# The rotary part of attention scores: two full passes become one full pass and a pair of 64-row passes

## The reference

```
q = concatenate([q_nope (128), rope(q_rope) (64)]);  k = concatenate([k_nope (128), rope(k_rope) (64, shared by the heads)])
s = einsum('bqhd,bkhd->bhqk', q, k) * scale
p = softmax(s);  out = einsum('bhqk,bkhd->bqhd', p, v)
```

## Time and profile before

| | us |
|---|---|
| runs of the kernel | 2785.1, 2790.86, 2793.07; median 2790.86 |
| span of the profiled execution | 2784.8 |
| median of the runs less that span | 6.1 |
| attention, from its first score matmul to its end | 829 to 1460 of the span |
| PE busy in the whole span | 2312.8 (83%) |
| PE, DVE, ACT, POOL busy in those 631 us | 606.0, 456.5, 355.7, 190.6 |

### The profile page before, as it was taken

One profiled execution on the slowest core, in us unless ns is written; L12 is line 12 of the kernel. 1 busy time (PEld: TensorE's weight loads), 2 busy tenths in 40 slices (PEclk: granted clock), 3 DMA queues, 4 the chain that ended last, 5 costly groups with the idle time before them and its releaser, 6 DMA issues. The chain is left out here.

```text
span 2784.8 us, 35274 instructions
## 1 busy us (share of the span) xinstructions
PE 2312.8 (83%) x11378; PEld 1915.8 (69%) x11378; DVE 1741.2 (63%) x2128; ACT 1102.2 (40%) x2062; POOL 1070.8 (38%) x711
## 2 busy tenths in 40 slices
PE   0899989999968999999988997949657765942998
PEld 0788868888856877787776885737546654732886
DVE  7233344444436777777762123799999999997432
ACT  2444433222225555555544555322332432341332
POOL 5222211222233333323311232747745855771444
PEclk9999989999989999999998998969878888975999
DMA  6333434434434333334214331010111011022553
GB/s 233 131 132 132 145 145 166 142 135 141 143 106 132 103 105 96 104 103 108 85 35 162 126 113 53 16 48 21 38 53 38 23 46 38 23 106 83 148 154 113
DMA packets 194607, 279.91 MB, mean 101 GB/s; under 512 B 10836, under 2 KB 139220, under 8 KB 189270
## 3 DMA queue, kind: packets, MB, share of 16 engines
q1 hardware_dynamic: 189910, 270.41, 30.2%
q10 hardware_dynamic: 4608, 8.39, 0.8%
HBM read 188.05 MB, written 90.70 MB: 100 GB/s over the span
## 5 line engine op out<-in xcount | busy, mean ns | idle before, releaser
L2062 DVE SCALAR_TENSOR_TENSOR conv_v<-u,par,conv_v 128x1024 f32<-128x1024 f32 x334 | 716.8, 2219 | 0.0
L2093 PE MATMUL ps<-ho_hi,wp_lo 128*128 128x512 f32 x768 | 314.3, 409 | 227.7 <-ACT gate L1985 164.8
L1950 POOL TENSOR_TENSOR conv_g<-conv_g,product 128x1024 f32<-128x1024 f32 x130 | 428.8, 3334 | 184.8 <-ACT product L1979 184.8
L2093 PEld LDWEIGHTS ps<-ho_hi,wp_lo 128*128 128x128 f32 x768 | 152.3, 198 | 266.0 <-issue 152.4
L2094 PE MATMUL ps<-h_left,wp_hi 128*128 128x512 f32 x768 | 310.8, 405 | 0.0
L2095 PE MATMUL ps<-ho_hi,wp_hi 128*128 128x512 f32 x768 | 310.0, 404 | 0.0
L1414 DVE TENSOR_TENSOR pt_lo<-ps_pt,pt_hi 128x512 fp32r<-128x512 f32 x256 | 175.8, 688 | 116.2 <-ACT pt_hi L1315 113.0
L1315 ACT ACTIVATE pt_hi<-ps_pt 128x512 fp32r<-128x512 f32 x256 | 154.0, 602 | 200.8 <-PE ps_pt L1496 199.3
L1979 ACT ACTIVATE product<-u,par 128x1024 f32<-128x1024 f32 x130 | 148.0, 1149 | 202.6 <-POOL conv_g L1950 201.7
L1404 DVE TENSOR_REDUCE mx<-ps_s 128x1 f32<-128x512 f32 x256 | 173.2, 684 | 39.7 <-PE ps_s L1488 38.7
L1308 ACT ACTIVATE probs<-ps_s,bias 128x512 f32<-128x512 f32 x256 | 173.8, 697 | 22.9 <-DVE bias L1410 15.2
(11 more groups left out here) (342 smaller groups left out, 5698.1 us busy)
## 6 DMA issues: line engine op xcount, KB each, us to landing
scratch_ret_pack<-pack SPq DMA_DIRECT2D x16, 1280.0 KB, 5.4
pack<-scratch_ret_pack SPq DMA_DIRECT2D x16, 1280.0 KB, 6.6
k_st<-scratch_k_t SPq DMA_DIRECT2D x64, 256.0 KB, 3.5
v_st<-scratch_v SPq DMA_DIRECT2D x64, 256.0 KB, 3.7
ada<-in_ada_w_dram SPq DMA_DIRECT2D x16, 768.0 KB, 6.1
w_st<-in_od_w_in_dram SPq DMA_DIRECT2D x24, 512.0 KB, 3.7
ada<-in_ada_w_dram SPq DMA_DIRECT2D x8, 1024.0 KB, 5.5
xt<-in_x_dram SPq DMA_DIRECT2D x16, 512.0 KB, 6.4
```

The lines of the kernel that those rows point to most:

```text
L1950: pool.tensor_tensor(half(conv_g, h), half(conv_g, h), product[h][:], ALU.add).then_inc(added, 1)
L2062: ins = dve.scalar_tensor_tensor(half(conv_v, h), units(k, h), w, half(conv_v, h), ALU.mult, ALU.add)
L2093: pe.matmul(dst, lo[:, k, :], h_hi[:, k, t], start=k == 0, stop=False)
```

## The change

The matmul `q_rot` by `kr_same` of 128 rows is taken out of `scores`. In its place stand, for each pair of key blocks (0 and 1, then 2 and 3), two matmuls of 64 rows, high by high alone: the one of the first bank reads partitions 0 to 63 (`q_rot` by `kr_same`), the one of the second reads partitions 64 to 127 (`q_up` by `kr_swap`). `q_up` is a new copy of the rotary query's high half on the upper partitions, kept in the upper half of `kr_same`, which needs no low half of the key any more. The term low by low is left out. The pair of banks 0 and 1 closes them, after scores 1 and before turn 1; the pair of banks 2 and 3 opens them, after turn 1, once the exponentials have freed both banks (`room`).

```
-                dve.tensor_copy(q_rot[sl][:], qr_st[:]).then_inc(rot_hi, 1)
+                dve.tensor_copy(q_up[sl], qr_st[ROPE:P, :]).then_inc(rot_hi, 1)
+                dve.tensor_copy(q_rot[sl][0:ROPE, :], qr_st[0:ROPE, :]).then_inc(rot_ready, 1)
                 dve.tensor_copy(q_hi[sl][:], q_st[:]).then_inc(qhi_done, 1)
                 hold(dve, st, rot_hi, m + 1)
-                dve.tensor_tensor(q_rot[sl][ROPE:P, :], qr_st[ROPE:P, :], q_rot[sl][ROPE:P, :].bitcast(F32),
+                dve.tensor_tensor(q_rot[sl][ROPE:P, :], qr_st[ROPE:P, :], q_up[sl].bitcast(F32),
                                   ALU.subtract).then_inc(rot_ready, 1)
...
-            dve.tensor_tensor(kr_same[ROPE:P, :], probs[0][0][ROPE:P, :], kr_same[ROPE:P, :].bitcast(F32),
-                              ALU.subtract).then_inc(kr_ready, 1)
             dve.tensor_tensor(kr_swap[0:ROPE, :], probs[0][0][0:ROPE, :], kr_swap[0:ROPE, :].bitcast(F32),
                               ALU.subtract).then_inc(kr_ready, 1)
...
+            def room(n, b, kb):
+                if not (isinstance(n, int) and n == 0 and b == 0):
+                    pe.wait_ge(exp_done, 16 * n + 4 * b + kb - 3)
...
-                pe.matmul(dst, q_lo[s][:, q], k_hi[s][:, k], start=True, stop=False)
+                pe.matmul(dst, q_lo[s][:, q], k_hi[s][:, k], start=opens, stop=False)
                 pe.matmul(dst, q_hi[s][:, q], k_lo[s][:, k], start=False, stop=False)
                 pe.matmul(dst, q_rot[s][:, q], kr_swap[:, k], start=False, stop=False)
-                pe.matmul(dst, q_rot[s][:, q], kr_same[:, k], start=False, stop=False)
-                pe.matmul(dst, q_hi[s][:, q], k_hi[s][:, k], start=False, stop=True).then_inc(s_done, 1)
+                mm = pe.matmul(dst, q_hi[s][:, q], k_hi[s][:, k], start=False, stop=not opens)
+                if not opens:
+                    mm.then_inc(s_done, 1)
+
+            def rope_pair(s, b, kb, opens):
+                q = slice(b * P, (b + 1) * P)
+                for half, q_hi_rot, k_rot in ((0, q_rot[s][0:ROPE, q], kr_same), (1, q_up[s][:, q], kr_swap)):
+                    rows, k = slice(half * ROPE, (half + 1) * ROPE), slice((kb + half) * BANK, (kb + half + 1) * BANK)
+                    mm = pe.matmul(ps_s[kb + half][:], q_hi_rot, k_rot[rows, k], start=opens, stop=not opens)
+                    if not opens:
+                        mm.then_inc(s_done, 1)
...
                     if score:
-                        scores(n, s, b, 0)
+                        scores(n, s, b, 0, True)
                     turn_next(0)
                     if score:
-                        scores(n, s, b, 1)
+                        scores(n, s, b, 1, True)
+                        rope_pair(s, b, 0, False)
                     turn_next(1)
                     if score:
-                        scores(n, s, b, 2)
-                        scores(n, s, b, 3)
+                        room(n, b, 2)
+                        room(n, b, 3)
+                        rope_pair(s, b, 2, True)
+                        scores(n, s, b, 2, False)
+                        scores(n, s, b, 3, False)
```

More of the change, by code:

```diff
@@ L1136, in attention @@
         kr_same, kr_swap = [sb(f"kr_{x}", [P, S], F32R) for x in ("same", "swap")]
+        q_up = [kr_same[ROPE:P, i * GQ:(i + 1) * GQ] for i in range(2)]
         q_hi = [sb(f"q_hi{i}", [P, GQ], F32R) for i in range(2)]
@@ L1177, in attention @@
         kr_hi = sem("kr_hi")
+        kr_turned = sem("kr_turned")
         kr_ready = sem("kr_ready")
@@ L1261, in group @@
                         hold(sp, st, q_ready, n + 1)
-                        hold(sp, st, rot_ready, n + 1)
+                        hold(sp, st, rot_ready, 2 * n + 2)
                         load_q(n + 1)
@@ L1343, in _ @@
             act.wait_ge(kr_in, 32)
-            act.activation(kr_same[:], probs[0][0][:], ACT.Copy).then_inc(kr_hi, 1)
+            act.activation(kr_same[0:ROPE, :], probs[0][0][0:ROPE, :], ACT.Copy).then_inc(kr_hi, 1)
             for q in range(QB):
                 split_k(0, 0, q)
-            act.wait_ge(kr_ready, 2)
+            act.wait_ge(kr_ready, 1)
             over_groups(act, group)
@@ L1461, in _ @@
             dve.wait_ge(kr_in, 32)
-            dve.tensor_copy(kr_swap[:], probs[0][0][:]).then_inc(kr_hi, 1)
+            dve.tensor_copy(kr_swap[:], probs[0][0][:]).then_inc(kr_turned, 1)
             split_q(0, 0)
-            dve.wait_ge(kr_hi, 2)
-            dve.tensor_tensor(kr_same[ROPE:P, :], probs[0][0][ROPE:P, :], kr_same[ROPE:P, :].bitcast(F32),
-                              ALU.subtract).then_inc(kr_ready, 1)
+            dve.wait_ge(kr_turned, 1)
             dve.tensor_tensor(kr_swap[0:ROPE, :], probs[0][0][0:ROPE, :], kr_swap[0:ROPE, :].bitcast(F32),
@@ L1473, in _, with scores @@
         def _(pe):
-            def scores(n, s, b, kb):
+            def room(n, b, kb):
+                if not (isinstance(n, int) and n == 0 and b == 0):
+                    pe.wait_ge(exp_done, 16 * n + 4 * b + kb - 3)
+            def scores(n, s, b, kb, opens):
                 if b == 0:
@@ L1478, in scores @@
                     pe.wait_ge(q_ready, n + 1)
-                    pe.wait_ge(rot_ready, n + 1)
-                if not (isinstance(n, int) and n == 0 and b == 0):
-                    pe.wait_ge(exp_done, 16 * n + 4 * b + kb - 3)
+                    pe.wait_ge(rot_ready, 2 * n + 2)
+                if opens:
+                    room(n, b, kb)
                 q, k = slice(b * P, (b + 1) * P), slice(kb * BANK, (kb + 1) * BANK)
                 dst = ps_s[kb][:]
-                pe.matmul(dst, q_lo[s][:, q], k_hi[s][:, k], start=True, stop=False)
+                pe.matmul(dst, q_lo[s][:, q], k_hi[s][:, k], start=opens, stop=False)
                 pe.matmul(dst, q_hi[s][:, q], k_lo[s][:, k], start=False, stop=False)
                 pe.matmul(dst, q_rot[s][:, q], kr_swap[:, k], start=False, stop=False)
-                pe.matmul(dst, q_rot[s][:, q], kr_same[:, k], start=False, stop=False)
-                pe.matmul(dst, q_hi[s][:, q], k_hi[s][:, k], start=False, stop=True).then_inc(s_done, 1)
+                mm = pe.matmul(dst, q_hi[s][:, q], k_hi[s][:, k], start=False, stop=not opens)
[8 more added lines that the diff above has]
+                        mm.then_inc(s_done, 1)
             def turn(m, sl, kt):
@@ L1546, in group @@
                         mm.then_inc(o_turned, 1)
-            pe.wait_ge(kr_ready, 2)
+            pe.wait_ge(kr_ready, 1)
+            pe.wait_ge(kr_hi, 1)
             over_groups(pe, group)
```

## The result

The changed kernel takes 2810.8 us (median of 4 runs, 2808.05 to 2814.24), the kernel before 2791.59 us beside it (4 runs): ratio 1.0077, 95% interval 1.0062 to 1.0092. It is 19 us slower; the forecast was 2810 against 2790.9, +19. The profiled execution has a span of 2805.9 us, 21.1 more than the earlier trace rows.

What follows compares the result with a forecast made beforehand. TensorE's order of matmuls was taken to bound attention. Terms +20.1 - 0.3 + 2.2 - 3.0 = +19.0 us on a span of 2784.8 gave 2803.8, plus 6.1 to the median: 2810 us, range 2786 to 2838.

Steps and rivals of the forecast that it cites:

- Price of a pair: Each pair in the 59 blocks with a turn: 0.23 + 0.40 - 0.46 = +0.17 us, over 118 pairs +20.1 us.
- Side by side: Two 64-row matmuls of 512 columns on the two partition halves run together: 0.23 us a pair, bounds 0.23 and 0.46.
- Five first blocks: Group 0 and the first block of group 1, without a turn between pairs, share one change in and out: -0.3 us.
- Wait of turn 1 in block 2: TensorE's wait for VectorE's low half of turn 3 grows by 0.16 us in 14 groups: +2.2 us.
- the copy, 0.33: The extra copy over 64 partitions in VectorE's query split takes 0.33 us, bounds 0 and 1.53.
- The start: Before the first scores, the low half in kr_same (3.36 us) goes and the extra copy adds 0.33: -3.0 us.
- The sum: Whole kernel: +20.1 - 0.3 + 2.2 - 3.0 = +19.0 us, a span of 2803.8 us.
- Late maxima: On VectorE, maximum 0 and the work behind it move back some 1.6 us in each block; cost put at nothing.

Runs made afterwards that it cites:

- whole rows in the pair's place: Changed kernel with each pair of 64-row matmuls replaced by two 128-row matmuls (q_rot by kr_swap), order, waits and copies kept: 2793.2 us, ratio 1.0018.
- the unpaired pass: Kernel before with one line changed: the pass q_rot by kr_same reads only partitions 0 to 63, in its old place: 2902.7 us, ratio 1.0409.
- adjacent pairs: Changed kernel with the second pair moved ahead of turn 1, right behind the first, one change in and out per block: 2782.5 us, ratio 0.998.
- Adjacent pairs with the later subtraction: Changed kernel with both pairs ahead of turn 1 and the query split's subtraction moved behind the low half of turn 3: 2780.2 us, ratio 0.9974.
- with the earlier split: Changed kernel with both pairs ahead of turn 1 and the whole query split moved ahead of low half 2 of block 1: 2784.3 us, ratio 0.9983.

## Why the prediction was right, step by step

**Price of a pair.** Forecast +0.17, measured +0.165 in most blocks 3 and 0.14 to 0.165 in blocks 0 and 1; over all 118 pairs it is some 18.8 us, against 20.1. Right, and for the reason given: whole rows in the pair's place take the loss away, the unpaired pass has twice the changes and pays 0.41 for each way in and out, adjacent pairs halve them. The rows of 128 columns in another stage gave the price of a change at 512 columns.

**Side by side.** Right: the starts coincide, and with both on one half of the rows each pair costs 0.215 more.

**Five first blocks.** Forecast -0.3, measured -0.15.

**Wait of turn 1 in block 2.** The mechanism was right, the size too small. Block 2 grew by 0.60, of which 0.33 are its pairs: 0.27 and not 0.16, some 4 us in place of 2.2. The term that was mis-sized is the copy, 0.33: VectorE's timeline in the changed kernel has the two 64-partition copies 0.45 apart. Ahead of the first scores, where no copy meets GpSimd, the first is 0.46 ahead of the second, and the second 0.34 ahead of `q_hi`; why the first costs more, no run isolates.

```profile
990.33 0.69 DVE L1417 TENSOR_TENSOR pt_lo<-ps_pt,pt_hi 128x512 fp32r<-128x512 f32 x1 [1.24 <-ACT pt_hi L1317]
...
991.48 0.43 DVE L1398 CAST kr_same<-qr_st 64x512 fp32r<-64x512 f32 x1
991.93 1.40 DVE L1399 CAST q_rot<-qr_st 64x512 fp32r<-64x512 f32 x1
993.26 0.41 DVE L1400 CAST q_hi<-q_st 128x512 fp32r<-128x512 f32 x1
...
994.42 0.69 DVE L1417 TENSOR_TENSOR pt_lo<-ps_pt,pt_hi 128x512 fp32r<-128x512 f32 x1
```

Whichever copy runs beside GpSimd takes 1.4 to 1.5, once, as assumed: now it is the second copy, and `q_hi` is down to 0.41.

**The start.** Forecast -3.0, measured -1.2: the first score matmul starts at 828.21, waiting for `k_lo`. In this execution the rotary key also reached VectorE 0.35 later (819.72, not 819.37), so the path from there to the first scores is 1.55 shorter, 8.49 for 10.04. The forecast's error was to take 2.06 us for each `k_lo` from a merged row. Narrower timelines of POOL have the first two by themselves; above the kernel before, below the changed one:

```profile
823.90 3.31 POOL L1355 TENSOR_TENSOR k_lo<-k_st,k_hi 128x512 fp32r<-128x512 f32 x1
...
827.17 3.32 POOL L1355 TENSOR_TENSOR k_lo<-k_st,k_hi 128x512 fp32r<-128x512 f32 x1
```

```profile
824.70 3.30 POOL L1357 TENSOR_TENSOR k_lo<-k_st,k_hi 128x512 fp32r<-128x512 f32 x1
```

The later ones take 1.3 (1293 ns is the median of six in the kernel before). In the kernel before, the two long ones stand beside VectorE's two long subtractions; in the changed kernel, with one subtraction, only the first is long, and it is the one that the scores wait for.

**The sum.** From the first score matmul to the end of attention the profiled execution grew by 22.4 us (pairs some 18.8, the wait of block 2 some 3.8, the five first blocks -0.15); less 1.2 at the start this is 21.2, and the span grew by 21.1. The forecast for the span was +19.0: the pairs came out 1.3 under it, the wait and the start together 3.4 over it. That the medians differ by 19.2, within 0.3 us of the forecast, is luck. The forecast put the median 6.1 above the span; it is 4.9 above in the changed kernel and 6.8 in the kernel before. Besides, the rotary key reaches VectorE anywhere from 818.2 to 822.6 us in the fourteen profiled executions, so a start 1 us earlier or later is not told from chance by one of them.

**Late maxima.** Forecast at nothing, and nothing it was: waits for exponentials are the same 12.8 us. Adjacent pairs with the later subtraction, and with the earlier split, show how near the limit lay.

**What was not foreseen** is that the changed kernel stood one VectorE instruction away from another 14 us.

## What to carry to other kernels

Count changes between full and half rows, not the matmuls saved: here a way in and out cost 0.40 us, nearly two full passes of 512 columns (0.23 each), so a pair has to replace more than 0.63 us of full passes to gain, and pairs belong next to each other. Look for the price of a form in any stage that already uses it, and for durations on the path open merged rows, whose mean hides the long one. When a small edit inside or ahead of a hardware loop costs more than its parts, compare the packets of the instruction queues and the idle time that names nothing before looking for a wait. When work moves on one engine, look at what the other engine does at its new time: the same copy took 0.42 or 1.4 us.

## What the runs showed of the hardware

A change between 128-row and 64-row matmuls costs 0.20 us each way at 2.4 GHz: 0.10 ahead of the first matmul of the new form and 0.10 of a weight load that isn't hidden. It is the same at 128 and 512 columns. Two 64-row matmuls on different halves start together; two on the same half cost 0.215 more. Between 64-row pairs of the same form nothing is lost.

Where waits of 2 us stood between the blocks of group 0, four 64-row matmuls a block run one by one took the granted clock from 1.00, which it was with two pairs side by side, to 0.56 and 0.72 (both matmuls on one half, no more changes of rows than before) and to 0.50 (unpaired pass, four changes in and four out); the first cost some 10 us, the second some 15, beyond what the passes and changes themselves cost at 2.4 GHz.

VectorE's loop over two groups met gaps of up to 5.4 us at its turn when one instruction more stood ahead of it, with 62 instruction packets in place of 42; five packets came with each turn, two of them inside the gap.

Where an operation of VectorE and one of GpSimd ran at the same time, one of them or both took longer: a copy on VectorE 1.4 to 1.5 us instead of 0.42, a subtraction there 1.37 instead of 0.69, and GpSimd's `k_lo` 3.3 instead of 1.3 beside VectorE's subtractions over 2048 columns.
